# Where the recurrent input is split into two halves: in the recurrent stage, or in the projection ahead of it

## The reference, cut to what matters

```python
def _layer_a(x, conv_buf, h0, norm_g, w_in, cw, cb, w_gx, b_gx, w_ga, b_ga, lam, w_out):
    u = _rmsnorm(x, norm_g) @ w_in
    xb, gate = jnp.split(u, 2, axis=-1)
    xc, new_buf = _causal_conv(xb, conv_buf, cw, cb)
    h, h_last = _rglru(xc, h0, w_gx, b_gx, w_ga, b_ga, lam)
    y = (h * jax.nn.silu(gate.astype(jnp.float32))).astype(x.dtype) @ w_out
    return x + y, new_buf.astype(conv_buf.dtype), h_last.astype(h0.dtype)
```

## Time and profile before

| | us |
|---|---|
| median of three runs | 1575.58 |
| lowest and highest run | 1575.48, 1580.06 |
| the profiled execution, its own time | 1575.82 |
| its span in the profile | 1574.0 |
| PE busy | 1496.0 (95%) |
| DVE busy | 1140.5 (72%) |
| ACT busy | 711.8 (45%) |
| POOL busy | 300.4 (19%) |

### The profile page before, as it was taken

One profiled execution on the slowest core, in us unless ns is written; L12 is line 12 of the kernel. 1 busy time (PEld: TensorE's weight loads), 2 busy tenths in 40 slices (PEclk: granted clock), 3 DMA queues, 4 the chain that ended last, 5 costly groups with the idle time before them and its releaser, 6 DMA issues.

```text
span 1574.0 us, 31123 instructions
## 1 busy us (share of the span) xinstructions
PE 1496.0 (95%) x10752; PEld 1425.8 (91%) x10752; DVE 1140.5 (72%) x2228; ACT 711.8 (45%) x1579; POOL 300.4 (19%) x224
## 2 busy tenths in 40 slices
PE   7999999999699999999999999999986999999999
PEld 7999999999689999998899999999974788888888
DVE  7975555658899999998784664846548777777771
ACT  5431221237876777763363433424345444444440
POOL 0000000003455555552440000000221111111110
PEclk9999999999899999999999999999999999999999
DMA  6321221234333333335522212212532444333312
GB/s 236 122 96 62 70 84 45 87 119 147 122 100 103 107 101 93 111 108 185 165 84 60 84 56 65 69 51 86 159 116 70 110 117 116 91 103 91 108 48 81
DMA packets 161967, 158.45 MB, mean 101 GB/s; under 512 B 54832, under 2 KB 154928, under 8 KB 161840
## 3 DMA queue, kind: packets, MB, share of 16 engines
q1 hardware_dynamic: 149712, 147.44, 31.2%
q10 hardware_dynamic: 12128, 9.39, 1.8%
HBM read 102.68 MB, written 54.36 MB: 100 GB/s over the span
## 4 chain that ended last, share of the span: by engine, by line
PE 53%; DVE 11%; issue 4%; ACT 3%; DMA 1%; POOL 0%; DVEq 0%; SPq 0%; ACTq 0%; POOLq 0%
PE s_banks L660 23%; PE bank L1513 11%; PE bank L1238 5%; PE s_banks L1450 3%; DVE r_th L973 2%; PE s_banks L1207 2%; PE bank L1465 2%; PE bank L1495 2%; PE bank L644 2%; DVE r_x_hi L997 2%; ACT m_p L1693 1%; PE bank L1499 1%; PE bank L1221 1%; DVE r_x L993 1%; DVE m_nmax L1560 1%
## 5 line engine op out<-in xcount | busy, mean ns | idle before, releaser
L1693 ACT ACTIVATE m_p<-s_banks,m_nm 128x192 f32<-128x192 f32 (+2 forms) x264 | 106.1, 414 | 182.0 <-DVE m_nm L1564 181.8
L1513 PE MATMUL bank<-m_y_hi,w_hi_a 128*128 128x256 f32 (+1 forms) x512 | 150.5, 294 | 0.6 <-DVE m_out L1624 0.6
L1513 PE MATMUL bank<-m_y_lo,w_hi_a 128*128 128x256 f32 (+1 forms) x512 | 145.8, 285 | 0.0
L1513 PE MATMUL bank<-m_y_hi,w_lo_a 128*128 128x256 f32 (+1 forms) x512 | 145.8, 285 | 0.0
L1157 POOL TENSOR_TENSOR r_xc_lo<-r_xc,r_xc_hi 128x528 fp32r<-128x528 f32 x32 | 52.6, 1645 | 424.6 <-DVE r_xc_hi L943 424.6
L660 PE MATMUL s_banks<-b_hi,w_hi_a 128*128 128x352 f32 x384 | 132.1, 344 | 0.0
L487 ACT ACTIVATE a_out<-a_out 128x352 f32<-128x352 f32 x48 | 24.0, 500 | 227.4 <-DVE a_out L582 227.4
L660 PE MATMUL s_banks<-b_hi,w_lo_a 128*128 128x352 f32 x384 | 124.7, 325 | 0.0
L660 PE MATMUL s_banks<-b_lo,w_hi_a 128*128 128x352 f32 x384 | 124.6, 325 | 0.0
L541 DVE RECIPROCAL b_qstd<-b_qstd 128x352 f32<-128x352 f32 x48 | 112.6, 2346 | 7.1 <-ACT b_qstd L483 4.8
L660 PE MATMUL s_banks<-b_hi,w_hi_b 128*128 128x352 f32 x336 | 115.1, 342 | 0.0
(11 more groups left out here) (204 smaller groups left out, 4798.4 us busy)
## 6 DMA issues: line engine op xcount, KB each, us to landing
w_raw_a<-weights_dram SPq DMA_DIRECT2D x31, 512.0 KB, 4.4
w_raw_b<-weights_dram SPq DMA_DIRECT2D x20, 512.0 KB, 4.8
sga_dram<-a_out SPq DMA_DIRECT2D x48, 176.0 KB, 1.8
r_xc<-xc_dram SPq DMA_DIRECT2D x32, 264.0 KB, 2.9
r_sg<-sga_dram SPq DMA_DIRECT2D x32, 264.0 KB, 2.7
r_x<-xT_dram SPq DMA_DIRECT2D x64, 132.0 KB, 2.2
x_dram<-r_x SPq DMA_DIRECT2D x64, 132.0 KB, 1.8
b_x<-x_dram SPq DMA_DIRECT2D x48, 176.0 KB, 2.3
```

The source lines that it names most:

```text
L1513: mm = nc.tensor.matmul(out_bank(ts, blk)[:, 0:width], w[pw][:, kt * P:(kt + 1) * P], (m.y_hi, m.y_lo)[px][tp][:, kt, 0:width], start=(n = ...
L1693: nc.scalar.activation(m.p[:, q, k, v0:192], s_banks[:, 2 * q + e, bp * 192 + v0:(bp + 1) * 192], ACT.Exp, bias=m.nm[:, q, k:k + 1], accum ...
```

## The change

The split of the recurrent input moves from the recurrent stage to the projection.
- In the projection ACT copies each finished branch block to its high part `a_out_hi` in the branch's slot, after waiting for `conv_done`; DVE subtracts for the low part `a_out_lo` in the following gate slot (`branch_low`), after waiting for ACT's copy. SP stores both (`store_halves`), 176 KB each, to new arrays `xc_hi` and `xc_lo` in HBM. `a_out_lo` lies in the memory of `a_xb`, and so a branch block waits until the halves of the block two before it are stored.
- In the recurrent stage DVE's cast and POOL's subtraction are gone. SP loads both halves, 264 KB each, one turn ahead (`load_halves`), and PE's gate products wait for that load. The plain `r_xc` is still loaded, for `gated_input`, now into two buffers and in its own turn.
- The raw input of the projection has a ring of four blocks in place of eight (the first tile's blocks 4 to 7 go to a place of their own).

```diff
+            if not at_start(m, s):
+                need(eng, m.x_lo, NB * s + blk - 3)
+                need(eng, m.sq_done, NB * s + blk - 3)
...
+                        if gate and not m.heads:
+                            store_halves(eng, m, s, t, blk)
+
+            def store_halves(eng, m, s, t, blk):
+                eng.wait_ge(m.out_low, NB * t + blk + 1)
+                q = blk % 2
+                for half, name in ((m.out_hi, "xc_hi"), (m.out_lo, "xc_lo")):
+                    dst = A[name].rearrange("(b p) t -> p b t", p=P)
...
+                        eng.dma_start(dst[:, blk, cols(t * PT, PT)], half[:, q, 0:PT].bitcast(F32)).then_inc(m.halves_stored[q], 16)
 
             run_project(eng, m, body)
+            if not m.heads:
+                for q in range(2):
+                    eng.wait_ge(m.halves_stored[q], halves_before(PN, q))
...
+                    if known(s, 1, PN) and not m.heads and not gate:
+                        q, width = at % 2, conv_width(s)
+                        eng.wait_ge(m.conv_done, NB * t + at + 1)
+                        need(eng, m.halves_stored[q], halves_before(t, at))
+                        nc.scalar.activation(m.out_hi[:, q, 0:width], m.out[:, place(m, j), 0:width], ACT.Copy)\
+                          .then_inc(m.out_high, 1)
...
+            def branch_low(s, t, j):
+
+                blk = part(m, j)[1]
+                n, q, width = NB * t + blk, blk % 2, conv_width(s)
+                eng.wait_ge(m.out_high, n + 1)
+                eng.wait_ge(m.halo_set, n + 1)
+                nc.vector.tensor_tensor(m.out_lo[:, q, 0:width], m.out[:, place(m, j - 1), 0:width],
+                                        m.out_hi[:, q, 0:width].bitcast(F32), ALU.subtract).then_inc(m.out_low, 1)
...
                 need(eng, m.conv_done, n - 1)
+                need(eng, m.halves_stored[q], halves_before(t, blk))
...
             def load_branch(s, g):
-                need(eng, r.ix_done, NG * (s - 1) + g + 1)
-                eng.dma_start(r.xc[:, g, :, :], xc_src[:, 2 * g:2 * g + 2, cols(s * RT, RT)])\
-                   .then_inc(r.xc_loaded[g], 16)
+                n, q = NG * s + g, g % 2
+                need(eng, r.ix_done, n - 1)
+                eng.dma_start(r.xc[:, q, :, :], xc_src[:, 2 * g:2 * g + 2, cols(s * RT, RT)])\
+                   .then_inc(r.xc_loaded[q], 16)
+
+            def load_halves(s, g):
+                n, q = NG * s + g, g % 2
+                need(eng, r.gates_done, 4 * (n - 1))
+                for dst, src in ((r.xc_hi, xc_hi_src), (r.xc_lo, xc_lo_src)):
+                    eng.dma_start(dst[:, q, :, :], src[:, 2 * g:2 * g + 2, cols(s * RT, RT)])\
+                       .then_inc(r.halves_loaded[q], 16)
...
-                if ahead(s, par, g):
-                    high(*ahead(s, par, g))
...
-                if ahead(s, par, g):
-                    low(*ahead(s, par, g))
...
                 split(eng, U_GATE + g)
-                eng.wait_ge(r.xc_low, n + 1)
+                eng.wait_ge(r.halves_loaded[q], 32 * (2 * s + g // 2 + 1))
```

More of the change, by code:

```diff
@@ L176, in project_memory @@
                 m.extra = (w_hi_c, b(f"{tag}_w_lo", [P, extra, D], F32R), w_raw_c)
+                if not heads:
+                    with ExitStack() as raw:
+                        m.x_first = tensors(raw)(f"{tag}_x_first", [P, NB - 4, PT])
                 m.hi = [hi0, b(f"{tag}_hi1", [P, NB, PT], F32R)]
@@ L583, in body @@
                           .then_inc(m.evacuated, 1)
+                        if not m.heads:
+                            branch_low(s, t, j)
                         if m.heads and 3 <= j < NB:
@@ L870, in body @@
                     behind = back_pair(s, g + 1) if g < NG - 1 else back_pair(s + 1, 0)
-                    if g < 2 and known(s, 1, RN - 1):
-                        load_branch(s, g + 2)
-                    if g >= 2 and known(s, 0, RN - 2):
-                        load_branch(s + 1, g - 2)
+                    if ahead(s, par, g):
+                        load_halves(*ahead(s, par, g))
+                    if known(s, 0, RN - 1):
+                        load_branch(s, g)
                     if isinstance(s, int) and (s, g) == (RN - 1, 0):
@@ L908, in start @@
                     eng.wait_ge(a1.stored[place(a1, j)], stored_before(a1, 2, j))
-                for g in range(NG):
+                for g in range(2):
+                    eng.wait_ge(a1.halves_stored[g], halves_before(2, g))
+                for g in range(2):
+                    load_halves(0, g)
                     load_branch(0, g)
@@ L915, in start_gates, with third, fourth @@
                 load_gate(0, 1)
-            def second():
-                load_branch(1, 0)
-            def third():
-                load_branch(1, 1)
-                load_gate(0, 2)
-            def fourth():
-                load_branch(1, 2)
+            def third():
+                load_branch(0, 3)
+                load_gate(0, 2)
+                load_halves(1, 0)
+            def fourth():
+                load_branch(1, 0)
                 load_gate(0, 3)
-            project_sync(eng, a1, {(PN, 0): start, (PN, 1): start_gates, (PN, 7): second, (PN, 10): third,
-                                   (PN, 12): fourth})
+            project_sync(eng, a1, {(PN, 0): start, (PN, 1): start_gates, (PN, 4): lambda: load_halves(0, 2),
+                                   (PN, 7): lambda: load_branch(0, 2), (PN, 8): lambda: load_halves(0, 3),
+                                   (PN, 10): third, (PN, 12): fourth, (PN, 13): lambda: load_halves(1, 1)})
             load_gate(1, 0)
@@ L1182, in turn @@
                 one, two = lagged(s, par, g, 1), lagged(s, par, g, 2)
-                if isinstance(s, int) and (s, g) == (0, 0):
-                    low(0, 0)
-                if ahead(s, par, g):
-                    low(*ahead(s, par, g))
                 if two:
```

91 lines of the change are left out of this document (53 added, 38 removed).

## The result

| | before | changed |
|---|---|---|
| median of the runs, us | 1575.53 (4 runs) | 1552.95 (4 runs) |
| lowest and highest | 1574.71, 1580.06 | 1550.03, 1554.98 |
| profiled execution, its span | 1574.0 | 1551.0 |

The ratio is 0.985, with an interval from 0.9825 to 0.987. The change makes the kernel 22.6 us faster. The direction and the place were right, the size of one term was not. In the changed kernel `gates` is L1266, `out` L1298, `kv` L1281, the scan L1047 and `y_low` L1233.

What follows compares the result with a forecast made beforehand. The prediction took DVE's list to bound the recurrent stage and the seam, with PE nearly full. Steady part 14.0 plus seam 4.0 made 18.0 us, from 1575.6 to 1557.6; range for 8 in 10: 1553 to 1569.

Steps and rivals of the forecast that it cites:

- What the change removes: Recurrent stage: each DVE turn shrinks 1.4 us (cast 0.34, scan stall 1.07), 5.6 per tile, so PE becomes the bound.
- What PE gets back there: Recurrent stage, steady part: PE's waits behind DVE and POOL shrink, gaining 14.0 us, bounds 7.8 and 15.6.
- behind matmuls, not behind the scan: Recurrent stage: why only 0.5 of PE's 2.1 us of waits for `r_x_lo` was counted as gained.
- The seam: Between projection and recurrent stage: DVE's shorter list starts PE's first output product earlier, gaining 4.0 us, bounds -0.8 and +6.2.
- A tie, and no charge: At the seam: turn 6's halves land near 421 us, just when PE's gate product can start, so no cost.
- What is added in the projection: Projection: added subtractions and copies are free in steps 2 to 5; step 1 costs 1.3 us only without cover.
- the transfers: Recurrent stage: two more 264 KB loads per turn, issued some 11 us ahead, land in 3 to 6 us.
- The rivals: Alternatives to PE becoming the bound (0.70): another DVE instruction stalls (0.16), nothing beyond 0.3% (0.06), slower through late halves (0.08).
- The stall only moves: Recurrent stage: POOL's gating multiplication starts earlier and stalls another DVE instruction, giving 1567.8 us; chance 0.16.

Runs made afterwards that it cites:

- POOL's subtraction alone: Changed kernel with only a POOL subtraction of 528 columns put back per turn, turns 8 to 31, on a spare tile: 1560.8 us, ratio 0.991.
- the cast alone: Changed kernel with only a DVE cast of 528 columns put back per turn, turns 8 to 31, on a spare tile: 1554.9 us.
- both dummies: Changed kernel with a DVE cast and a POOL subtraction put back per turn, turns 8 to 31, results unread: 1568.9 us, ratio 0.996.
- two casts: Changed kernel with two DVE casts of 528 columns added per turn, turns 8 to 31, on a spare tile: 1562.0 us.
- three casts: Changed kernel with three DVE casts of 528 columns added per turn, turns 8 to 31, on a spare tile: 1572.2 us.
- four casts: Changed kernel with four dummy DVE casts added per turn, turns 8 to 31, no POOL instruction: 1581.9 us, ratio 1.005.
- the low part on DVE: Kernel before, with the recurrent input's low part subtracted by DVE behind its cast instead of by POOL: 1567.4 us, ratio 0.995.
- four casts in two turns: Changed kernel with four dummy DVE casts added only in the turns of groups 0 and 1 of tiles 2 to 7: 1562.3 us.
- The early load: Changed kernel with turn 6's halves loaded in the last projection step's slot 14, not behind the last stores: 1552.7 us, ratio 0.985.

## Why the time was missed, by the prediction's steps

**What the change removes (right, but not all of it).** The scan at 1.42 us, DVE with rests and PE as the bound, 42 us per tile: all as written. The run with POOL's subtraction alone shows the stall by itself, and the one with the cast alone that without the stall nearly nothing is won. DVE's busy time per tile was to fall by 5.6 us and fell by 8.4 (43.8 to 35.4). The prediction overlooked that the second `r_x_hi` and `r_sq` of two turns per tile stood still beside POOL as well, some 3.2 us, which go because DVE now rests at that place. The Trainium skill, "SBUF — State Buffer", section "SBUF: two separate sides", names the lock between VectorE and GpSimd for DVE instructions with two SBUF inputs or in a mode that uses both ports. The runs agree for the scan (1.42 us alone, 2.23 beside POOL) and for `r_sq` (0.43 and 1.55). `r_x_hi` has one tensor and a vector as its inputs and shows it too (0.36 us alone, 0.95 beside POOL); no run shows in which mode it works.

**What PE gets back there (the step that failed, in its size).** The prediction counted 13.5 us of wait rows as gained, 0.5 of the 2.1 for `r_x_lo`, and set the upper bound at 15.6, "all". Measured 20.2. Two things were off. First, all waits went, those for `r_x_lo` included: 1.6 more. The prediction had put them "behind matmuls, not behind the scan". But the stalled scan stands in the same list of DVE, and DVE runs from it to `r_x_lo` without a rest:

```profile
437.66 2.49 DVE L973 TENSOR_TENSOR_SCAN r_th<-r_a,h_last,r_ti 128x264 f32<-128x264 f32 x2
442.56 0.48 DVE L1002 SCALAR_TENSOR_TENSOR r_x_lo<-r_x,vec,r_x_hi 128x264 fp32r<-128x264 f32 x1
443.09 0.39 PE L1221 MATMUL bank<-r_x_hi,w_hi_a 128*128 128x264 f32 x1 [0.91 <-DVE r_x_lo L1002]
```

Secondly, 15.6 was not all. A wait row tells less than the hole costs. Here is PE before, around one wait of the earlier trace rows:

```profile
599.67 0.28 PE L1221 MATMUL bank<-r_x_lo,w_hi_a 128*128 128x264 f32 x1
599.79 0.28 PE L1221 MATMUL bank<-r_x_hi,w_lo_a 128*128 128x264 f32 x1
601.01 0.39 PE L1238 MATMUL bank<-r_y_hi,w_hi_a 128*128 128x264 f32 x1 [0.94 <-POOL r_y_lo L1170]
601.24 0.28 PE L1238 MATMUL bank<-r_y_lo,w_hi_a 128*128 128x264 f32 x1
```

Without a hole one matmul starts 0.12 us after the other. Here it is 1.22, so 1.10 is lost ahead of the first, while the row says 0.94: it counts from the end of the last matmul's 0.28 us, during which the next would already have begun. And the next starts 0.23 us later, another 0.11. The hole costs 1.21 us for a row of 0.94, 0.27 more. Fifteen of them make 4.1. So 15.6 + 4.1 = 19.7. The 0.5 that is left of 20.2 is the size of two holes that have no row at all, since they are shorter than the part of the last matmul that the row does not count. Here is one, the other lies at 458.74:

```profile
446.73 0.28 PE L1238 MATMUL bank<-r_y_hi,w_lo_b 128*128 128x264 f32 x1
447.01 0.39 PE L1221 MATMUL bank<-r_x_hi,w_hi_a 128*128 128x264 f32 x1
447.24 0.29 PE L1221 MATMUL bank<-r_x_lo,w_hi_a 128*128 128x264 f32 x1
```

It costs 0.16 + 0.11 = 0.27 us.

Other kernels agree, in tiles where the clock stays high. One tile, from a group's gate product to the same one of the next tile, against 41.69 in the changed kernel:

| kernel | tile | over 41.69 | rows of waits in it | rest per hole |
|---|---|---|---|---|
| before | 44.54 | 2.85 | 1.35 + 0.94 | 0.28 |
| both dummies | 43.93 | 2.24 | 1.19 + 0.51 | 0.27 |
| POOL alone | 42.88 | 1.19 | 0.93 | 0.26 |
| two casts | 42.91 | 1.22 | 0.94 | 0.28 |
| three casts | 44.39 | 2.70 | 1.28 + 0.92 | 0.25 |

With four casts it is 0.35 for each of four (558.98 to 605.38). In the tiles with the low part on DVE and with four casts in two turns it is more, 0.69 and 0.53 for one row each. All three have one more hole, without a row: between PE's matmuls at 592.00 and 592.32, at 593.30 and 593.74, and at 558.21 and 558.52. The count does not hold where the clock falls: in the tile of the two dummies around 517 us, and in the next tile of the four casts, 2.0 us are left over the two rows of each, and most of that is the slow matmuls named above.

**The seam (right, with some luck).** Forecast 4.0, measured 4.5 at the output product and 3.9 at gate product 6. Some 0.7 of both was there before the last step began: DVE's slot at 322.70 before starts at 322.02 now. The kernel before with the low part on DVE, which changes nothing up to there, shows 321.92, so that this is how two executions differ and not a gain. "A tie, and no charge" for the halves was right within 0.7 us: PE finished the product at 420.9, most of it at the low clock (granted 0.55 from 415.6 to 420.9), and waited 0.5 until 421.36. The early load shows that not even these count in full.

**What is added in the projection, and the transfers (right).** PE's waits in its first step are unchanged and there are none later. Halves land in 3.0 and 3.3 us, with a lead of 9 to 11, and PE waits for none of them behind turn 6. The plain `r_xc` takes 3.8 us now against 2.9, without a wait of PE for it in the steady part.

**Behind the last gate product (nothing forecast).** 1.1 us of 24.1 were given back there, most of it in the attention. Two executions of the changed kernel differ by as much: at 737.93 and 738.16 us they are 0.2 apart, at 1147.17 and 1148.37 they are 1.2 apart. So no run shows this as an effect of the change, and none shows that it is not.

**The rivals.** "The stall only moves" did not happen, but its mechanism is real. `r_x_hi` and `r_sq` stood still beside POOL in the kernel before, and do so again where casts fill DVE's rests. In the changed kernel DVE has less to do per tile than PE, so it waits for PE while POOL works, and does not meet it there. One stall stays in both kernels: the first `r_x_hi` of each turn, beside POOL's gating multiplication, takes 0.86 to 0.98 us in place of 0.36.

## What to carry to other kernels

A row of waits is a lower bound of what a hole in a dense row of matmuls costs: read the distance from start to start across it, take off the usual pitch, and do so again for the matmul behind it. Before giving an elementwise instruction to GpSimd, see which VectorE instructions lie beside it: here 0.75 us more on DVE was cheaper than 1.06 us of stall. And do not add up DVE's rests as room; look what POOL does in them, since added work first fills the rest and then stretches.

## What was not expected of the hardware

The stall is not a matter of the scan alone: `r_x_hi`, a TENSOR_SCALAR of 264 columns, takes 0.36 us or, beside POOL, 0.95 to 1.29, and `r_sq` 0.43 or 1.55. A matmul of 264 columns behind a hole of 1.34 us (612.55 in the kernel before) took 0.39 us and let the next one start after 0.23, at a granted clock of 1.00, against 0.28 and 0.12 in a dense row. Casts of 528 columns that each wait for the one before start every 0.47 us, while an instruction that does not wait starts 0.34 us behind one.
